# Reordering the first steps of a three-layer decoder kernel: the first projection unit ahead of the decay and beta columns, and one modulation row moved in between feature units

## The reference

```python
# layer 0: conv_gdn_mixer
proj = x @ w_in                                   # 8192 columns + 16: beta_raw, a_raw
h_a, c_a, b_a, z_a, qkv, z_b, beta_raw, a_raw = split(proj)
qkv = silu(causal_depthwise_conv(qkv, conv_b_w))
q, k = l2_normalize(q), l2_normalize(k)
beta = sigmoid(beta_raw)
g = -exp(a_log) * softplus(a_raw + dt_bias)       # the decay
o = gated_delta_rule(q, k, v, g, beta)            # starts from cumsum(g)
# layer 2: second_block
mod = silu(c) @ w_ada + b_ada                     # 6 x 1024 columns
sh1, sc1, g1, sh2, sc2, g2 = split(mod)
hn = rms(x) * (1 + sc1) + sh1
x = x + g1 * (mixer(hn) @ w_out)                  # mixer: features hn @ w_in, then attention
x = x + g2 * (silu(gate) * up) @ w_down           # on rms(x) * (1 + sc2) + sh2
```

## Time and profile before

| what | us |
| --- | --- |
| median of 3 runs | 1022.48 (1021.67 to 1025.93) |
| the profiled execution, whole | 1025.05 |
| its span, first to last instruction | 1023.2 |
| TensorE busy | 1003.1 |
| VectorE busy | 764.7 |
| ScalarE busy | 547.5 |
| mean granted TensorE clock | 0.994 of 2.4 GHz |

### The profile page before, as it was taken

The page is one execution under the profiler, slowest core; times in us unless marked ns, Lnnn a source line. Parts: engine busy times, 40 slices in busy tenths (PEclk is TensorE's granted clock), DMA queues, the critical chain, the costliest instruction groups (busy, mean ns, idle before and its releaser), DMA issues.

```text
span 1023.2 us, 19324 instructions
## 1 busy us (share of the span) xinstructions
PE 1003.1 (98%) x8144; PEld 845.2 (83%) x8144; DVE 764.7 (75%) x1121; ACT 547.5 (54%) x657; POOL 0.5 (0%) x7
## 2 busy tenths in 40 slices
PE   9999999999999999999999899999998999999998
PEld 7999999999876788888878777668976668888886
DVE  5998964797548768888898857866998776786534
ACT  6674543562443563575647246466976655455431
POOL 0000000000000000000000000000000000000000
PEclk8999999999999999999999999999999999999999
DMA  9453432442335774344334345877542348545441
GB/s 357 171 188 127 162 125 89 159 165 94 118 111 228 292 269 165 130 160 167 109 141 165 125 166 210 323 281 275 204 163 83 126 169 323 188 183 206 155 174 42
DMA packets 27188, 181.33 MB, mean 177 GB/s; under 512 B 3040, under 2 KB 4320, under 8 KB 5984
## 3 DMA queue, kind: packets, MB, share of 16 engines
q1 hardware_dynamic: 25056, 174.66, 46.0%
q10 hardware_dynamic: 2048, 5.45, 1.4%
HBM read 179.04 MB, written 1.05 MB: 176 GB/s over the span
## 4 chain that ended last, share of the span: by engine, by line
PE 92%; DVE 4%; ACT 1%; DMA 1%; issue 1%; POOL 0%; ACTq 0%; POOLq 0%
PE PS L955 88%; PE PS L1132 1%; DMA RAW<-wst 1%; DVE WL L1892 1%; PE PS L1210 1%; DVE layer_ln L2239 1%; PE PS L1059 0%; DVE block L2379 0%; PE PS L1364 0%; ACT block L1756 0%; ACT block L1762 0%; DVE block L2394 0%; DVE layer L2232 0%; DVE layer L2231 0%; PE PS L1249 0%
## 5 line engine op out<-in xcount | busy, mean ns | idle before, releaser
L955 PE MATMUL PS<-XHL,WH 128*128 128x512 f32 (+1 forms) x1808 | 504.6, 349 | 1.8 <-DVE layer L2178 1.3
L955 PE MATMUL PS<-XHL,WL 128*128 128x256 f32 x1392 | 392.4, 282 | 0.0
L1892 DVE TENSOR_TENSOR WL<-RAW,WH 128x2048 fp32r<-128x2048 f32 (+1 forms) x138 | 312.2, 2271 | 75.2 <-ACT WH L1443 75.0
L955 PEld LDWEIGHTS PS<-XHL,WH 128*128 128x128 f32 x1808 | 314.9, 191 | 47.2 <-issue 1.9
L1443 ACT ACTIVATE WH<-RAW 128x2048 fp32r<-128x2048 f32 x138 | 261.2, 1899 | 147.8 <-PE PS L955 135.9
L955 PEld LDWEIGHTS PS<-XHL,WL 128*128 128x128 f32 x1392 | 265.7, 191 | 0.9 <-issue 0.7
L955 PE MATMUL PS<-WH,XHL 128*128 128x512 f32 x320 | 104.0, 395 | 0.3 <-ACT XHL L1580 0.3
L955 PE MATMUL PS<-WH,YH 128*128 128x512 f32 x224 | 89.1, 398 | 0.0
L955 PE MATMUL PS<-WH,YL 128*128 128x512 f32 x224 | 87.4, 390 | 0.0
L955 PE MATMUL PS<-WL,YH 128*128 128x512 f32 x224 | 87.3, 390 | 0.0
L955 PEld LDWEIGHTS PS<-WH,XHL 128*128 128x128 f32 x320 | 60.1, 188 | 13.7 <-DVE WL L1892 0.7
...
## 6 DMA issues: line engine op xcount, KB each, us to landing
RAW<-wst SPq DMA_DIRECT2D x162, 1024.0 KB, 4.9
...
```

What stands on the lines that cost most here:

```text
L955: return pe.matmul(o, lhsT, rhs, start=start, stop=stop)
L1892: tt(WL[:, i % RAW_RING, 0:n], RAW[:, i % RAW_RING, 0:n], as_float(WH[:, k % SPLIT_RING, 0:n]), ALU.subtract).then_inc(vector_done, 1)
```

## The change

In `plan()` the modulation row `ada:4` is asked for after the feature `feat:3` instead of before the first feature; its two slabs are thereby loaded after those of feat 8, 1, 0, 2 and 3 (list positions 112 and 113 instead of 108 and 109), and the banks of some later steps change. All three tables are new. On TensorE `ba` stands behind the whole unit `k:0:0` instead of ahead of it. On ScalarE and VectorE the first half of x is split before the second, and before the second half of slab 0. On VectorE `split:1:1` stands ahead of `ba`. Further steps change places by one or two throughout layers 0 to 2; no step is added or taken away.

```diff
@@ plan() @@
     quarters(4)
-    ada(4)[0]()
+    end_row()
     step("wg2", on="V")
...
     root(0, 2)
+    ada(4)[0]()
     feat(4)
@@ ORDER_T @@
-ba first:k:0:0 k:0:0 first:k:0:1 k:0:1 first:v:0:0 v:0:0 norm:k:0 ...
+first:k:0:0 k:0:0 ba first:k:0:1 k:0:1 first:v:0:0 v:0:0 norm:k:0 ...
...
-... hd:0 first:i:0:1 i:0:1 hm:0:0 first:f:1:0 hm:0:1 f:1:0 hm:0:2 ...
+... hd:0 first:i:0:1 hm:0:0 i:0:1 hm:0:1 first:f:1:0 hm:0:2 f:1:0 hm:0:3 ...
...
-... ada:9:0 ada:9:1 ada:4:0 adat:7 xt:4:0 xt:4:1 xt:4:3 adat:9 xt:4:2 ada:4:1 first:feat:8 ...
+... ada:9:0 ada:9:1 adat:7 xt:4:0 xt:4:1 xt:4:2 adat:9 xt:4:3 first:feat:8 ...
@@ ORDER_S @@
-setup split_top xs:1 split:0:0 xs:0 split:1:1 ba1 split:2:2 ba2 c1 split:3:3 k:0:0 ...
+setup split_top xs:0 xs:1 split:0:0 split:1:1 ba1 split:2:2 ba2 c1 split:3:3 k:0:0 ...
@@ ORDER_V @@
-split_top xs:1 split:0:0 xs:0 ba split:1:1 split:2:2 ba1 ba2 k:0:0 split:3:3 k:0:1 ...
+split_top xs:0 xs:1 split:0:0 split:1:1 ba split:2:2 ba1 ba2 k:0:0 split:3:3 k:0:1 ...
```

More of the change, by code:

```diff
@@ L494 @@
 ORDER_T = """
[L495 to L524, removed]
@@ L533 @@
+down:1:3 down:1:4 first:down:1:5 down:1:5
 """
 ORDER_S = """
-setup split_top xs:1 split:0:0 xs:0 split:1:1 ba1 split:2:2 ba2 c1 split:3:3 k:0:0 split:4:4 k:0:1 split:5:5 norm:k:0
-v:0:0 split:7:7 split:6:6 v:0:1 split:8:8 q:0:0 q:0:1 split:9:9 low:zb:0:0 norm:q:0 gc:0 split:11:11 low:zb:0:1
-split:10:10 split:12:12 k:1:0 split:14:14 k:1:1 split:13:13 split:15:15 norm:k:1 v:1:0 v:1:1 split:16:16 ah:0:0
-gx:0:1:0 gx:0:1:1 split:18:18 split:17:17 q:1:0 low:az:0:0 split:19:19 zb:0:1 gx:0:2:0 q:1:1 gx:0:2:1 az:0:0
@@ L569 @@
-fl:18 split:126:152 ff:18 split:127:153 fl:19 fl:20 split:128:154 ff:19 fl:21 split:129:155 ff:20 split:130:156
-split:131:157 split:132:158 ff:21 split:133:159 split:134:160 split:136:162 split:135:161 split:137:163 split:138:164
+setup split_top xs:0 xs:1 split:0:0 split:1:1 ba1 split:2:2 ba2 c1 split:3:3 k:0:0 split:4:4 k:0:1 split:5:5 norm:k:0
+v:0:0 split:7:7 split:6:6 v:0:1 q:0:0 q:0:1 split:8:8 low:zb:0:0 split:9:9 norm:q:0 low:zb:0:1 gc:0 split:10:10 k:1:0
+split:11:11 split:12:12 k:1:1 split:13:13 split:14:14 split:15:15 norm:k:1 v:1:0 v:1:1 gx:0:1:0 split:16:16 gx:0:1:1
@@ L571 @@
+fl:14 split:122:148 fl:15 ff:14 split:123:149 ff:15 fl:16 fl:17 split:124:150 split:125:151 ff:16 fl:18 ff:17
+split:126:152 ff:18 fl:19 split:127:153 split:128:154 ff:19 fl:20 split:129:155 fl:21 split:130:156 ff:20
+split:131:157 ff:21 split:133:159 split:134:160 split:132:158 split:136:162 split:135:161 split:137:163 split:138:164
 """
 ORDER_V = """
-split_top xs:1 split:0:0 xs:0 ba split:1:1 split:2:2 ba1 ba2 k:0:0 split:3:3 k:0:1 setup split:4:4 split:5:5 v:0:0
-norm:k:0 gcc v:0:1 q:0:0 split:6:6 q:0:1 split:7:7 split:8:8 sum:zb:0:0 gc:0 split:9:9 norm:q:0 gc2:0 k:1:0 sum:zb:0:1
@@ L615 @@
-fs:20 split:128:154 ff:19 split:129:155 split:130:156 ff:20 fs:21 split:131:157 split:133:159 split:132:158 ff:21
-split:134:160 split:135:161 split:136:162 first:down:0:5 split:137:163 down:0:5 split:138:164 first:down:1:5 down:1:5
+split_top xs:0 xs:1 split:0:0 split:1:1 ba split:2:2 ba1 ba2 k:0:0 split:3:3 k:0:1 setup split:4:4 split:5:5 v:0:0
+norm:k:0 gcc v:0:1 q:0:0 split:6:6 q:0:1 split:7:7 gc:0 split:8:8 sum:zb:0:0 split:9:9 norm:q:0 sum:zb:0:1 gk:0 k:1:0
+vtr:0 gc2:0 split:11:11 split:10:10 gkk:0 wg k:1:1 gp:0:0:0 split:12:12 gp:0:0:1 gu:0:0:1 gu:0:0:0 v:1:0 gp:0:1:0
@@ new lines @@
+split:72:79 sum:q1:3:0 split:73:80 hl:2:0 f:3:1 sum:q1:3:1 hz:2 split:74:81 hy:3:0 hd:3 hr:2:0 hp:3:0 hy:3:1
+split:75:82 hy:3:2 hp:3:1 hy:3:3 hp:3:2 split:76:85 hy:3:4 sum:z1:3:0 hp:3:3 hy:3:5 sum:z1:3:1 hp:3:5 split:78:87
+hp:3:4 hy:3:6 split:77:86 hy:3:7 split:79:88 hp:3:6 adat:3 hl:3:0 hl:3:1 split:80:89 hz:3 split:81:90 split:82:91
+mod:0 hr:3:0 split:83:92 hr:3:1 first:out:1:1:3 first:out:1:0:3 lna:1:0 lnb:1:0:0 out:1:0:3 out:1:1:3 lna:1:1
+lnb:1:0:1 lnb:1:1:0 xt:2:0:0 split:84:98 adat:8 lnb:1:1:1 xt:2:1:0 xt:2:0:1 split:85:99 xt:2:1:1 split:86:100
@@ L617 @@
+ff:21 split:132:158 split:134:160 first:down:0:5 down:0:5 split:135:161 split:136:162 split:138:164 split:137:163
+first:down:1:5 down:1:5
 """
```

180 lines of the change are left out of this document (102 added, 78 removed).

## The result

| what | before | after |
| --- | --- | --- |
| median, us | 1022.48 (1021.13 to 1025.93, 9 runs) | 1031.16 (1028.16 to 1033.65, 9 runs) |
| the profiled execution, whole | 1025.05 | 1028.16 |
| its span | 1023.2 | 1026.4 |
| mean granted clock | 0.994 | 0.997 |

The changed kernel is slower: the ratio is 1.0072, with a 95% interval from 1.0059 to 1.0086, which is 7.4 us (6.0 to 8.8). The difference of the medians is 8.7. The forecast was +7.9 us and 1030.4. The profiled execution is the shortest of its nine, 3.0 us under their median.

What follows compares the result with a forecast made beforehand. TensorE's work plus its own waits was taken to bound the kernel (busy 1003.1 of 1023.2 us). Terms 5.9 + 1.9 + 0.5 - 0.4 = +7.9 us on the 1022.5 median gave 1030.4, range 1023.5 to 1035.

Steps and rivals of the forecast that it cites:

- The first unit at 10.4: Start of TensorE: first:k:0:0 starts at 10.4 instead of 13.24, 2.8 us earlier, once x's first half is split.
- The clock in the first unit: Start: the granted clock falls at 10.9 and rises at 14.9, so the first unit ends at 18.1.
- The end of `ba`, 21.7 (19.7 to 22.9): Start: ba ends at 21.7; 19.7 if the clock never falls, 22.9 if it falls 2.4 us into ba.
- The queue, 16.7 us: VectorE and ScalarE steps queued behind ba take 16.7 us from its end until norm:k:0 can start.
- The wait, 5.3 us (3.5 to 5.5 as the sign): Ahead of norm:k:0: TensorE has 11.4 us of work, runs dry at 33.1 and waits some 5.3 us.
- `norm:k:0` at 38.4: First layer: norm:k:0 starts at 38.4 instead of 32.56, +5.9 us, between +3.9 and +7.1.
- The low clock behind the wait, +1.9 (0 to 2.2): Behind TensorE's wait for norm:k:0: the clock drops to half speed for a stretch, costing +1.9 us, between 0 and 2.2.
- `ada:4`, +0.5 (-0.5 to +1.5): Third layer's features: first feature 0.5 us sooner, ada:4's 2.0 us still to do, partly absorbed by attention waits: +0.5 us.
- The other places, -0.4: First HGRN2 group: the 0.39 us wait before hm:0:1 goes because hm:0:0 moves ahead of a half unit: -0.4 us.
- swaps 0 (3 either way): Remaining swaps of neighbouring steps cost nothing while a half unit still covers them: 0, 3 us either way.
- The rival of the short wait: Start: clock stays up, ba ends at 19.7, norm:k:0 is 3.9 us late; sum +4.0, 1026.5 us; chance 20%.
- that of the new waits: Clock falls within ba, low clock costs 2.2, ada:4 1.5, swaps lose 3: +13.4, 1035.9 us; chance 10%.

Runs made afterwards that it cites:

- the start alone: Kernel before with first:k:0:0 and k:0:0 ahead of ba, x split earlier and split:1:1 ahead of ba on VectorE: 1029.76 us, ratio 1.0057.
- the kernel that keeps TensorE at work: Changed kernel with four products of ones put ahead of norm:k:0, where TensorE had stood still: 1031.62 us, ratio 1.0075.
- The row alone: Kernel before with only ada:4 moved behind first:feat:4, ScalarE copying it ahead of qn:0:1: 1025.24 us, ratio 1.0015; with the copy behind qn:0:1, 1031.36 us.

## Why the prediction was right

The forecast was 1030.4 with a range from 1023.5 to 1035.0. The median is 1031.16. By its own steps:

- **The first unit at 10.4.** It starts at 10.39 in the change and between 10.33 and 10.43 in every kernel with that start.
- **The clock in the first unit.** Taken: a fall at 10.9, the unit ends at 18.1. In both profiles of the changed kernel it did not fall, and in the first the unit ended at 16.21; in five of the eight profiles with this order it fell and the unit ended near 17.7. The forecast took one case for the rule.
- **The end of `ba`, 21.7 (19.7 to 22.9).** 19.85 in the profile of the change, 21.37 in that of the start alone. It is within the bounds each time, near the lower one in the changed kernel.
- **The queue, 16.7 us.** Measured 16.66 and 16.65, and 16.66 again in the second profile; the forecast took the durations from the rows of before and nothing else. The rule of the Trainium skill (ScalarE: Activation LUTs, What ACT_TABLE_LOAD costs) with its drain on top would have made it longer by some 1.0 us; these rows speak against it once more (in the profile of the change the load at 25.99 takes 1.28 us, and the next instruction starts 0.01 behind it).
- **The wait, 5.3 us (3.5 to 5.5 as the sign), and `norm:k:0` at 38.4.** The wait was 3.56 to 3.57 us in both profiles of the change and in the start alone; `norm:k:0` starts at 36.51 and 38.02. Of the wait, the step that failed is the term of TensorE's work between: it was 13.1 us in the profile (19.85 to 32.95), not 11.4, since the clock falls during or right behind `ba`. The prediction had that only as a case within `ba`. It costs 1.7 us that the wait then takes up, so it makes the wait shorter and nothing later.
- **The low clock behind the wait, +1.9 (0 to 2.2).** Not there in the first profile, 1.44 us in the second, 1.4 to 1.6 by the kernel that keeps TensorE at work, 1.8 in the start alone. The prediction had called itself wrong if the clock stayed at 1.0 behind the wait. In the first profile it did; of the four profiles with this wait that is one. The Trainium skill (TensorE: Matmul & The Clock Gate, HAM oscillation) has the block behind such a wait for data start cold every time. Here it was cold in three of four, so as a rule for every execution it is too strong for 3.6 us.
- **`ada:4`, +0.5 (-0.5 to +1.5).** This term was mis-sized. The row alone is +1.5 us by time. In the profile of the change the gain ahead of the features is 0.6 us as forecast, but the 2.0 us of the row stay whole, and the stretch is 2.80 us longer. With the row alone it is 2.2 longer, so by these profiles 0.6 come from the swaps in the attention; the waits for VectorE (L2396) are in every kernel with the change's tables for it and in none with those of before. The step that failed is that the waits of the attention would take the row up: with the row alone they have the sizes of before (1.00, 0.90, 0.37 and 0.39 us against 0.99, 0.90, 0.37 and 0.39) and only come later.
- **The other places, -0.4, swaps 0 (3 either way).** The wait of 0.39 us of the earlier trace rows, before `hm:0:1`, is gone, but one of 0.47 stands two levels later (408.22), and one of 0.89 in the second group, so the -0.4 was not gained, and the second layer is 0.6 us longer. The first layer is 0.6 shorter. The swaps cancel, within the bound.

By terms: for the start 7.8 us were forecast (5.9 and 1.9). It was 3.95 in the first profile of the change, 5.4 in the second, 7.3 in that of the start alone, in which the clock fell at the first unit and behind the wait, as forecast. For all the rest +0.1 was forecast, and it was +2.2 in the first profile. The mechanism of the start, the queue behind `ba`, is right. That the sum comes so near the median is luck in part, since these two errors had opposite signs. The rival of the short wait describes the first profile (+4.0 at the start, the clock up), but not the median, and that of the new waits was right on `ada:4`.

One thing does not close. The changed kernel with the old start is at +3.1 us (1.8 to 4.3). The row (+1.5) and the first layer's order (-1.3) leave 2.9 for the order of the second layer and of the attention, in which the profiles show 0.6 and 0.6. Over all fourteen profiles the second layer's stretch in the table is 230.2 to 230.4 us with the change's order and 228.9 to 230.3 without, 0.8 more on average. The intervals are wide enough to hold the rest; it may also be that these orders make the low clock near 530 more frequent, which three of seven profiles with them show and none of the seven without. That was not tested.
